# A two-layer diffusion trunk step on one core: where the shift is added, how the last combination is laid out, and when one group of modulation weights is multiplied

## The reference

```python
def modulation(cond, w, b):
    m = jax.nn.silu(cond) @ w + b               # (1024) @ (1024, 6144), one per condition and layer
    return jnp.split(m[:, None, :], 6, axis=-1)
for l in range(DEPTH):
    mp, ms = modulation(c_ctx, ada_w[l], ada_b[l]), modulation(c, ada_w[l], ada_b[l])
    hp = modulate(rms_norm(xp, norm_mix[l]), mp[0], mp[1])      # h * (1 + scale) + shift
    hs = modulate(rms_norm(xs, norm_mix[l]), ms[0], ms[1])
    yp, ys = mixer(hp), mixer(hs)
    xp, xs = xp + mp[2] * yp, xs + ms[2] * ys
    hp = modulate(rms_norm(xp, norm_ffn[l]), mp[3], mp[4])
    hs = modulate(rms_norm(xs, norm_ffn[l]), ms[3], ms[4])
    xp, xs = xp + mp[5] * hier_moe(hp), xs + ms[5] * hier_moe(hs)
# hier_moe: softmax over 4 groups (top 1), then over its 8 experts (top 2);
# y = sum over the two experts of weight * ((silu(x @ Wa) * (x @ Wb)) @ Wd)
```

## Time and profile before

| | us |
|---|---|
| median of 3 runs (1394.18 to 1398.1) | 1394.41 |
| profiled execution | 1396.16 |
| its span | 1394.3 |
| PE busy | 1235.7 |
| DVE, ACT, POOL busy | 549.2, 380.5, 414.4 |
| mean granted clock of PE | 0.942 |

### The profile page before, as it was taken

One profiled execution on the slowest core, in us unless ns is written; L12 is line 12 of the kernel. 1 busy time (PEld: TensorE's weight loads), 2 busy tenths in 40 slices (PEclk: granted clock), 3 DMA queues, 4 the chain that ended last, 5 costly groups with the idle time before them and its releaser, 6 DMA issues.

```text
span 1394.3 us, 21214 instructions
## 1 busy us (share of the span) xinstructions
PE 1235.7 (89%) x7039; PEld 797.8 (57%) x7040; DVE 549.2 (39%) x1254; ACT 380.5 (27%) x779; POOL 414.4 (30%) x741
## 2 busy tenths in 40 slices
PE   6999998989989579998784899999999399999877
PEld 5666777655567345554443766665676255555437
DVE  3121424676622732222111449998213622222214
ACT  2210036556511311111110345664313011111110
POOL 0300100300000334453333159986001324445420
PEclk9999999989999779999997899999799599999998
DMA  9775653010036569999984911113552689999965
GB/s 379 269 255 210 260 216 134 3 61 1 1 39 233 228 261 411 423 424 423 423 356 173 273 58 38 57 61 102 116 205 112 261 334 408 369 421 423 423 247 227
DMA packets 104678, 324.77 MB, mean 233 GB/s; under 512 B 20405, under 2 KB 54171, under 8 KB 82083
## 3 DMA queue, kind: packets, MB, share of 16 engines
q1 hardware_dynamic: 84016, 290.36, 53.9%
q0 software_dynamic: 12464, 21.91, 4.4%
q10 hardware_dynamic: 8131, 11.59, 2.3%
HBM read 314.52 MB, written 27.10 MB: 245 GB/s over the span
## 4 chain that ended last, share of the span: by engine, by line
PE 65%; SPq 9%; DMA 9%; DVE 7%; issue 5%; ACT 2%; POOL 2%; ACTq 0%; POOLq 0%; DVEq 0%
PE PS L687 10%; PE PS L1043 10%; PE PS L1170 10%; PE PS L733 8%; PE PS L1065 5%; SPq L548 4%; DMA arena<-in_moe_w_up 4%; SPq L551 3%; PE PS L1111 3%; PE PS L640 3%; DVE scratch L1645 3%; PE PS L919 3%; DMA ring<-in_ada_w 2%; PE PS L1028 2%; DMA ring<-in_moe_w_up 2%
## 5 line engine op out<-in xcount | busy, mean ns | idle before, releaser
L1645 DVE TENSOR_TENSOR arena<-arena,PS 128x128 f32<-128x128 f32 (+3 forms) x109 | 40.3, 386 | 299.7 <-ACT arena L1540 288.8
L1043 PE MATMUL PS<-ring,arena 128*64 128x256 f32 x1088 | 132.3, 395 | 15.1 <-DMA ring<-in_moe_w_up 13.3
L733 PE MATMUL PS<-ring,arena 128*128 128x256 f32 (+1 forms) x640 | 143.3, 378 | 1.7 <-ACT arena L1352 1.7
L1170 PE MATMUL PS<-arena,ring 128*128 128x320 f32 x512 | 141.7, 438 | 3.5 <-issue 2.2
L1043 PE MATMUL PS<-arena 128*64 128x256 f32 x1120 | 130.6, 383 | 15.3 <-DMA arena<-in_moe_w_up 14.2
L2424 POOL TENSOR_TENSOR arena<-arena 128x655 f32<-128x655 f32 x91 | 129.7, 1425 | 45.2 <-ACT arena L1611 32.1
L687 PE MATMUL PS<-arena,ring 128*128 128x320 f32 x512 | 138.3, 433 | 4.8 <-DVE arena L1933 3.7
L733 PEld LDWEIGHTS PS<-ring,arena 128*128 128x128 f32 x640 | 116.3, 193 | 30.1 <-issue 15.3
L1170 PEld LDWEIGHTS PS<-arena,ring 128*128 128x128 f32 x512 | 97.7, 192 | 47.3 <-issue 8.6
L687 PEld LDWEIGHTS PS<-arena,ring 128*128 128x128 f32 x512 | 97.1, 190 | 45.6 <-issue 5.4
L2185 DVE SCALAR_TENSOR_TENSOR PS<-arena,vecT,PS 128x655 f32<-128x655 f32 x124 | 112.1, 904 | 4.2
(11 more groups left out here) (342 smaller groups left out, 1633.9 us busy)
## 6 DMA issues: line engine op xcount, KB each, us to landing
ring<-in_moe_w_up SPq DMA_DIRECT2D x64, 1024.0 KB, 15.1
arena<-in_moe_w_up SPq DMA_DIRECT2D x64, 1024.0 KB, 18.3
ring<-in_ada_w SPq DMA_DIRECT2D x48, 1024.0 KB, 9.0
ring<-in_moe_w_down SPq DMA_DIRECT2D x32, 1024.0 KB, 16.2
arena<-in_moe_w_down SPq DMA_DIRECT2D x32, 1024.0 KB, 18.5
arena<-y_rows ACTq DMA_DIRECT2D x10, 1024.0 KB, 8.0
ring<-in_od_w_in SPq DMA_DIRECT2D x16, 512.0 KB, 6.3
ring<-in_ev_w_in SPq DMA_DIRECT2D x7, 1024.0 KB, 15.6
```

Of the source, the lines that this page charges most:

```text
L733: last = pe.matmul(z_bank(i)[:, 0:n], hT[:, k, t * P:t * P + P], w[:, k, 0:n], start=(k == 0), stop=(k == KD - 1))
L1043: last = pe.matmul(PS[i * BLK:(i + 1) * BLK, 0, 0:2 * P].rearrange("p (a n) -> p a n", a=2), xblk[:, k, :], w[:, k % 4, :, i * P:(i + 1) * P],
L1170: last = pe.matmul(PS[:, 2 * a + n, 0:SEG], w[:, k, a, :], hT[:, k, n * SEG:(n + 1) * SEG], start=(k == 0), stop=(k == KD - 1))
L1645: return dve.tensor_tensor(out, a, b, op)
```

## The change

1. *The shift leaves POOL.* The latent tokens' shift is added by DVE where it copied rows into `xblk`: `take_rows` becomes an add of `shift_x`, a table of 128x8, and POOL's five adds go. For the context tile, PE adds the difference of the two shifts (`delta`) into the same PSUM bank: `cdiag` is a diagonal of the root, which the later scaling by the reciprocal root cancels. Its transposes become matmuls with the identity, with one matmul of 512 columns more for each half.
2. *The router's shift.* `router_bias` goes. ACT writes the shifts as two more columns of `xA` (tokens 640 and 641), `raw_logits` carries them, two more selecting matmuls bring them out, and DVE forms `lbias` as the first step of the routing.
3. *POOL's block loop.* Index columns are copied before the waits, the gather goes ahead of the wait for the block's output, and in the tail one copy takes all four columns, without a wait for each scatter to land.
4. *Group 4 of the modulation.* The slices 32 to 39 are no longer multiplied beside the input projection, but behind the last expert of layer 0. They have slots 6, 7, 8, 0, 1, 2, 15 and 16; SP may fill these once experts 26, 27 and 29 are done. PE waits for the bias (`mod_c`) before it combines.
5. *Norm behind layer 0's experts.* POOL adds a tile's eight blocks of squares to one (three adds) for four of the five tiles, so that `tile_sum` is one matmul. Sum and spread move back by one step of the loop, ACT squares in halves.
6. *End of layer 1.* `xT` is turned to token order before the combination, and DVE copies it to `xout`. The combination stays in token order: for features 0 to 511 two matmuls of 512 columns (`combine_rows`), for 512 to 1023 ACT and DVE scale and add; DVE multiplies both by a broadcast row of the gate and adds `xout`.

```diff
 def ada_beside(i):
     g, r = 1 + i // 8, i % 8
-    return [] if r == 0 or g == 5 else [8 * g + r - 1] if r < 7 else [8 * g + 6, 8 * g + 7]
+    return [] if r == 0 or g >= 4 else [8 * g + r - 1] if r < 7 else [8 * g + 6, 8 * g + 7]
+BACK_SLOTS = (6, 7, 8, 0, 1, 2, 15, 16)
...
     plan += [("expert0", i) for i in range(PER_EXPERT * EXPERTS)]
+    plan += [ada(m) for m in range(4 * KD, 5 * KD)]
     plan += [("od_in", j) for j in range(8)]
...
# PE
-            def router_bias(l, b):
-                for c in range(2):
-                    for k in range(KD):
-                        last = pe.matmul(PS[:, b, ROUTE * c:ROUTE * (c + 1)], bc(modT[:, l, 24 + k, c:c + 1], [P, P]), wr[:, k, :],
-                                         start=(k == 0), stop=(k == KD - 1))
...
+                    for c in range(2):
+                        last = pe.matmul(PS[:, 6, (NT + c) * ROUTE:(NT + c + 1) * ROUTE], bc(rs[0:PAIR, T + c:T + c + 1], [PAIR, P]),
+                                         cst[0:PAIR, C_SEL:C_SEL + ROUTE], start=True, stop=True)
...
+                    if t == ST:
+                        pe.wait_ge(ev("shift_dma"), 64 * (l + 1))
+                        pe.wait_ge(ev("cdiag"), l + 1)
+                        last = pe.matmul(PS[:, b, :], cdiag, delta_row[:, 512 * half:512 * half + 512], start=False, stop=True)
...
+                if l == 0:
+                    for n in range(4 * KD, 5 * KD):
+                        modulation(n)
+                    mod_columns(4)
+                    pe.wait_ge(ev("mod_c"), MODC + 5)
...
+                def combine_rows(s):
...
+                    for a in range(2):
+                        last = pe.matmul(PS[:, 4 + s % 4, :], wdiag[:, a, t, :], ygat[:, t, a, 0:512],
+                                         start=(a == 0), stop=(a == 1))
...
-                for s in range(NT + 2):
+                if l == 1:
+                    turn_x()
+                    for s in range(NT):
+                        combine_rows(s)
+                    return
+                for s in range(NT + 3):
                     if s < NT:
                         combine(s)
...
+                    if 2 <= s <= NT + 1:
+                        tile_sum(s - 2)
+                    if s >= 3:
+                        spread(s - 3)
...
# DVE
-                    dve.tensor_copy(xblk.rearrange("p (c m) n -> p m c n", c=2),
-                                    quad(3).rearrange("p m (c n) -> p m c n", c=2)).then_inc(ev(f"xblk_c{l}"), 1)
+                    tt(xblk.rearrange("p (c m) n -> p m c n", c=2), quad(3).rearrange("p m (c n) -> p m c n", c=2),
+                       bc(shift_x[:, :].rearrange("p (c m) -> p m c", c=2).unsqueeze(3), [P, 4, 2, BLK]), ALU.add) \
+                        .then_inc(ev(f"xblk_c{l}"), 1)
...
+                def rows_out(s):
...
+                    dve.wait_ge(ev("xt_a"), s + 1)
+                    dve.scalar_tensor_tensor(out=upper, in0=upper, scalar=wtok[:, 1, t:t + 1], in1=ygat[:, t, 0, 512:D],
+                                             op0=ALU.mult, op1=ALU.add)
+                    dve.wait_ge(ev("comb_mm"), 2 * NT + s + 1)
+                    link(tt(lower, PS[:, 4 + s % 4, :], gate_row[:, c, 0:512], ALU.mult))
+                    tt(upper, upper, gate_row[:, c, 512:D], ALU.mult)
+                    link(tt(xout[:, t, 0:512], xout[:, t, 0:512], lower, ALU.add))
+                    tt(xout[:, t, 512:D], xout[:, t, 512:D], upper, ALU.add).then_inc(ev("comb"), 1)
...
# POOL
-                for t in range(NT):
-                    pool.wait_ge(ev("htok_a"), 2 * NT * l + 2 * (t + 1))
-                    pool.tensor_tensor(htok[:, t, :], htok[:, t, :], shift[0 if t < ST else 1], ALU.add) \
-                        .then_inc(ev("h_tok"), 1)
...
                 for r in range(LAND):
-                    if r < 2:
-                        landed(r, laps + 2)
                     pool.wait_ge(ev(f"yblk_c{l}"), 4 * laps + (LAND + r + 2))
-                    columns(r, laps, 4 * laps + (r + 1), False)
-                    scatter(r, scatter_col[:, r:r + 1])
-                    freed((r - 1) % LAND, laps + (0 if r == 0 else 1))
+                    settle(4 * r + 3)
+                    scatter(r, gather_col[:, r:r + 1])
...
+            for s in range(NT - 1):
+                pool.wait_ge(ev("squared"), KD + s + 1)
+                for n in (4, 2, 1):
+                    t = cols(TILES[s])
+                    ins = pool.tensor_tensor(hT[:, 0:n, t], hT[:, 0:n, t], hT[:, n:2 * n, t], ALU.add)
```

243 lines of the change are left out of this document (146 added, 97 removed).

## The result

| | before | after |
|---|---|---|
| median | 1394.74 us | 1360.05 us |
| range of 4 runs | 1394.18 to 1398.1 | 1357.74 to 1360.18 |
| profiled execution, its span | 1396.16, 1394.3 | 1357.74, 1355.3 |
| mean granted clock | 0.942 | 0.95 |

The ratio is 0.9742 (95% interval 0.9724 to 0.9761): 34.7 us less by the medians. The forecast was 1350.2, in a range of 1337 to 1366.

What follows compares the result with a forecast made beforehand. Weights set layer 0's expert stage; elsewhere the chain of waits leaves PE at four places the change touches. Terms 8.8 + 5.0 + 2 x 8.5 + 1.4 + 4.5 + 7.5 = 44.2 us saved: median 1350.2, range 1337 to 1366.

Steps and rivals of the forecast that it cites:

- The front: Up to the heads: removing eight modulation slices and four transposes saves 8.8 us, between 7 and 9.9.
- Router bias of layer 0: Layer 0's head loop: removing the bias matmuls saves 5.0 us, between 3.5 and 7, partly through the clock.
- Dispatch: Routing in both layers: without POOL's adds DVE's small operations shorten, saving 8.5 us per layer, between 6.5 and 9.3.
- The tail of layer 0: Behind layer 0's experts, through the tile loop: 1.4 us saved, between 8 lost and 6 saved.
- The rival of the collision: Layer 0's tail: last slices share queues with the outputs, losing 8 us instead of saving 1.4; 1360 us, chance 0.20.
- 2.7 + 1: Layer 0's tile loop: 2.7 us saved by the later sum and spread, 1 us by slices warming the clock.
- Layer 1 ahead of the projection: Before layer 1's output projection: removing the router bias saves 4.5 us, between 3 and 7.
- My lower value: Layer 1's output projection: 4.5 us instead of 6.9, as 6 us at half speed would lose 3.
- The end: Layer 1's last combination and output: DVE sets the pace at 3.5 us a tile; 7.5 us saved, between 5 and 11.
- The slow case: Heads and attention: the clock stays on its lower level, so the kernel is slower than before; 1420 us, chance 0.03.
- the case that the dispatch gain is not carried through: Experts of both layers: late first weights or rows lose both 8.5 us; 1367 us, chance 0.08.
- the case that the clock stays up: Upper ends come out at four places, both tails included, 12.6 us more saved; 1338 us, chance 0.11.

Runs made afterwards that it cites:

- e1: Kernel after with modulation slices 32 to 39 multiplied beside the input projection again, not behind layer 0's last expert; ratio 0.9788 to the kernel before.
- e5: Kernel after with the old tile loop: eight matmuls per tile sum, spread and norm a step earlier, no POOL sums; ratio 0.9754 to the kernel before.
- e4: Kernel after with the router bias's 32 matmuls of 36 columns back at both old places, result unused; ratio 0.9843 to the kernel before.
- e2: Kernel after, but in both layers the sixth place's weights (3 MB) load only once the first two gathers have landed; ratio 0.971 to the kernel before.
- v1: Kernel after with five of eight slices loaded behind the outputs, and the sixth place's weights waiting for the first gathers; 1339.49 us, ratio 0.9596 to before.
- e3: Kernel after with five POOL adds of 128x1024 at each layer's dispatch, into a buffer nobody reads; ratio 0.9788 to the kernel before.
- v3: v1 with the gate's rows written to HBM ahead of the fourth place's weights in layer 1; 1337.47 us, ratio 0.9585 to the kernel before.
- v2: v1 without the sixth place's wait for the gathers, so only the five late slices; ratio 0.9635 to the kernel before.
- e6: Kernel after with one slice's weights multiplied five more times, unused, where PE waited in layer 0's tile loop; ratio 0.9721 to the kernel before.
- v4: v3 with one slice behind the last expert and seven behind the outputs; ratio 0.9652 to the kernel before.

## Why the prediction was right in kind and 10 us too low

Against the profiled execution the forecast was 5.2 us too much saved (44.2 against 39.0), against the medians 9.5. The difference of the two is that after was profiled in its fastest execution and before in one above its median.

**The front**: 12.0 instead of 8.8. The step that failed was that the chain would pass to ACT near 214 us and give some of the 9.9 back. PE waits 4.4 us for DVE there in both kernels (4.37 and 4.40), and nothing passed on; e1 and e5, which have the same dip of the clock, give 10.5. The other 1.5 us isn't shown: after has no dip at 112 to 120 us, but one at 32 to 48 (0.88 and 0.91), and this front takes 232.4 to 235.7 us in the executions here.

**Router bias of layer 0**: 5.5 for 5.0, the size by luck, since the reading was wrong. I put the lower level down to the run of small matmuls; e4 has the run and not the level, and the run alone is worth 2.2.

**Dispatch**: 8.3 and 8.3 for 8.5. Mechanism, next wait (ACT's exponential) and size held. Only one thing was misread: of DVE's small operations beside POOL's adds, those with two inputs ended with an add, while the reductions took 0.17 us (469.43 in before). What failed is the sentence behind it, that the expert stage would simply begin earlier. I compared the rows' writing with the gather's start, found room (11 us; it is 7.8), and overlooked that the weights of the last two places, issued behind that writing, were still in the queues when the gather came 7.8 us behind their first issue instead of 14.0. 3.1 and 2.2 us went there; e2 gives them back, and more.

**The tail of layer 0**: -4.4 for +1.4. POOL's shorter tail gave the forecast 3.6 us (3.5 in e1), and the last scatter of POOL's loop landed under load as reckoned, 12.9 us behind the last weights' use against 12.7. The failed step is the next: I let POOL go on when the scatter with data had landed. It waits for all four, and the last, issued 4.2 us later without data, lands 6.5 us after its issue too. The 2.1 us of the earlier trace rows are of an idle queue; what counts is who else is in the engines, not whether the scatter has data. The rival of the collision (8 us lost, 1360) isn't what happened either: it had the last slices beside the outputs' fetch, and the slices were through by then (DMA share 0.15 ahead of 733.90). They collided with the scatters. That its median is the one measured is luck. One of my own signs of being wrong did come, PE waiting for the bias, but it cost 0.1 us at most. In the tile loop I had 2.7 + 1. The 2.7 is near the 2 us that v1's loop shows with the clock up; the 1 us had the wrong sign. The clock was lower in the last 10 us, not higher, and took most of it, which left 0.5 (0.8 against e5).

**Layer 1 ahead of the projection**: 6.9 for 4.5. I took the level to rise at the same moment of the program with or without the run. Without it the level rose some 8 us earlier in the module, 2.5 us ahead of the projection, and e4, with the run back, loses all of 7.1 and 2.0 more behind it. My lower value had no support but the timing of one execution. What I feared does occur: in e1 and e3, also without the run, the level rises 3 us into the projection. It costs 1.6 us there, not 3.

**The end**: the first combination 1.3 us later instead of 0.5 sooner, the rest 7.5 for 7.0. DVE's 3.3 us a tile was reckoned at 3.5. v3 finds the 1.3 us, and more: the gate's broadcasts beside the last scatter, a transfer of the change that I had not costed.

The slow case is out: attention is as long as it was. Of the case that the dispatch gain is not carried through, about a third came, 5.4 of 17 us, by the late gather. Of the case that the clock stays up, one of four places came out, the 6.9 us in layer 1; in both tails it didn't.

Left open: why the low level at the end of layer 1's convolution module lasts 3.4 us in v1, v2 and v3, some 14 in after (both times), e2 and e5, 17 in e6 and v4, 20 in e1 and e3, and 27 in e4. Neither the start of the stage (v4's is v1's) nor a tile loop at full clock (e6's last 10 us) decides it, and no run here separates what does. Of v1's 20 us, 6 hang on it. What sets the place of the dips in the front isn't known either.

## What to carry to other kernels

When a chain gets shorter, look at what is in the DMA queues at the new moment: four of this case's misses (two gathers, scatters with slices, scatters with a broadcast) are small transfers that someone waits for, issued into a stream that nobody waits for yet. The stream could wait here: holding it back until the small transfer had landed, with the slices and the gate's rows moved, gave 22 us (1337 against 1360), of which 6 are the clock's in the convolution module and not explained. And bulk loads moved into a gap are free only if nothing with a short deadline has to pass through the same gap.

Compare kernels by stage starts before believing a total: here most untouched stages repeat within 0.3 us, while the total moves by 2 to 6. Look at the clock in each stage too: two stages (front and layer 1's output projection) moved by 2 to 3 us with it and without an edit.

## What the runs showed of the hardware

A gather's rows took 6.9 us with 6 MB of weights issued up to 8 us ahead of it, and 3.0 with the later 3 MB held back. Scatters took 6.5 to 6.7 us beside slices and 2.1 to 2.8 without, also when they carry no data. The Trainium skill (DMA: Bandwidth & Descriptors, Queues, rings and completion order) has the DMA engines take turns between queues packet by packet; the trace agrees as far as both advance, and shows the price for the small one.

DVE operations of 20 columns with two inputs took up to 1.85 us beside POOL adds of 128x1024 (2.0 us each) that share no data with them, and reductions beside the same adds 0.17 to 0.20. The Trainium skill (SBUF — State Buffer, Who interferes with whom) has two-input operations that read SBUF twice contend with a GpSimd that reads, and reductions never on trn2; the trace agrees on both. In the prediction I cited only that page's rule for copies and scalars, for DVE's diagonals in the tile loop; they took 0.29 us each, and none met one of POOL's sums in time.

The granted clock of the same matmuls differs between executions and kernels without any edit nearby: 0.79 at 112 to 120 us in four of thirteen executions, 0.84 to 0.94 at 32 to 48 us in four others, and from 3.4 to 27 us at 0.50 at the end of one module of layer 1. Idle PE time filled with matmuls kept the mean at 0.92 instead of 0.50 for 10 us; the next stage was 1.8 us shorter.
